# A two-block transformer kernel on one core: another order of work around the joined pair, and the joining copies on VectorE

## The chip, the cores and the metric

One Trainium2 chip, one of its cores. The metric is the device time of one execution in microseconds (us), the median of several runs. The engines are TensorE (PE, with its weight loads as PEld), VectorE (DVE), ScalarE (ACT), GpSimd (POOL) and SyncE (SP), which here issues nearly all the DMAs.

## The reference

256 tokens of width 1024 in float32 run through two layers of a first block (feed-forward, mixer, feed-forward) and two layers of a second one (mixer, cross attention, feed-forward). The change touches only the feed-forwards, of which there are six:

```
def swiglu_ffn(h, w_gate, w_up, w_down):
    return (jax.nn.silu(h @ w_gate) * (h @ w_up)) @ w_down
```

`h` is 256 x 1024, the hidden width is 2816, and every result is normalised and added to `x`.

## The kernel before

Every float32 product is made of three products of rounded parts: an operand is a high part (`w_hi`, `hT_hi`: rounded by a copy on ScalarE) and a low part (`w_lo`, `hT_lo`: operand minus high part, by a subtraction on VectorE), and TensorE multiplies high by high, high by low and low by high into the same PSUM bank. So each weight tile of 128 x 2048 passes through four hands: SyncE loads it into one of five `raw` buffers (`unit`, line 531), ScalarE makes its high part (`high`, line 1420, four buffers), VectorE its low part (`weight_low`, line 2112), and TensorE multiplies both in 24 matmuls of 512 columns (lines 738 and 875) and so frees them. Such a tile with its matmuls is a unit.

A feed-forward runs over 11 chunks of 256 hidden columns. A plain chunk has two units of gate and up weights, and one for the down projection, which TensorE multiplies one chunk later. Between them the hidden values are made: `silu` on ScalarE, `hidden` (the product with the up half) on VectorE, then the turning of the hidden tile by DMA transposes of 16-bit values. For it VectorE splits the float32 values into their upper and lower 16 bits (`part`, line 2208), SyncE issues two transposes (`turn_halves`, lines 571 and 567), and two copies of 128 x 512 uint16 put the halves together again in the buffer `joined` (`join_here` on ScalarE, line 1527, or `join` on VectorE, by the switch `JOIN_ON_ACT`). ScalarE rounds `joined` to the high part (`hidden_high`, line 1532), VectorE makes the low part (`hidden_low`, line 2203), and the down unit can be multiplied. `hidden` on ScalarE stands for `join_here` and `hidden_high` together.

Chunks 5 and 6 form a joined pair (`PAIRS = (5,)`): their gate and up products are made by seven smaller block products in place of eight, with sums of operands. VectorE makes the sums of rows (`rows_whole`, `row_sums`, `row_sums_low`, lines 2245 and 2247) during chunks 2 to 4, and the sums of weight blocks `t1` (line 2259), `t2` (2264), `t4` (2271) and `t3` (2275). TensorE multiplies the blocks in the order 1, 5, 2, 6, then the down unit of chunk 4, then 3, 7, 4. The text calls their units p1, p5, p2 and so on. `t1` needs p1 and p7 loaded, `t4` needs p2. `hold` (line 1585) copies the finished blocks 1 and 5 out of PSUM. Chunk 7 stands behind the pair (`chunk_behind`): TensorE multiplies its two units, then the down unit of chunk 5 (down 5) and that of chunk 6 (down 6). The hidden values of chunk 6 have buffers of their own: the halves in line 567, and `second_hi`, `second_lo`, which a profile shows as `form_lo`.

Each engine runs its instructions in the order in which they are written; nothing is scheduled at run time. So an engine that waits for one thing holds up all that is written behind it. The orders are in `chunk`, `chunk_behind` and `pair`, once for each engine. `low(n)` and `high(n)` below are the low and the high part of unit n of a feed-forward (11, 12: chunk 4; 13: down 3; 14: p1; 15: p5; 16: p2; 17: p6; 18: down 4; 24: down 5; 25: down 6; 26, 27: chunk 8; 28: down 7).

Of the kernel before, what the change touches and what calls it, by code (L numbers as in the profile page):

```python
# [45 lines left out]
AHEAD = HIGH_RING - 1  # L46
# [12 lines left out]


PAIRS = (5,)
JOIN_ON_ACT = True
HOOK = 7


# [140 lines left out]
def _program(ctx, nc, d, out, counted):  # L206
# [309 lines left out]
    def _(sp):  # L516
# [30 lines left out]
        def gate_up(L, k, kh, wg, wu, c):  # L547

            dst = raw[:, SLOT[L.unit(k)], :].rearrange("p (k g n) -> p k g n", k=4, g=2)
            halves = []  # L550
            for g, w in enumerate((wg, wu)):
                src = w[bass.ds(L.l, 1), 512 * kh:512 * kh + 512, bass.ds(c * FC, FC)]
                halves.append((dst[:, :, g, :], src.rearrange("o (k p) n -> p (o k) n", p=P)))
            unit(L, k, halves)
# [7 lines left out]
        def turn_halves(L, n, c):  # L562

            sp.wait_ge(halves_ready, L.turns(n, c))
            if c in SECOND:
                for t in range(TT):
                    sp.dma_start_transpose(second_halves_T[:, t, :, :],  # L567
                                           second_halves[:, t, :, :].rearrange("p b n -> p (b n)")).then_inc(second_turned, 16)
                return
            for t in range(TT):  # L570
                sp.dma_start_transpose(halves_T[:, t, :, :], halves[:, t, :, :].rearrange("p b n -> p (b n)")).then_inc(
                    halves_turned, 16)

        def ffn(L, n, k0, wg, wu, wd, ffn_ahead=None):
            for kh in range(2):
                gate_up(L, k0 + kh, kh, wg, wu, 0)
            if ffn_ahead:
                turn_halves(*ffn_ahead, NCHUNK - 1)

            def chunk(c):  # L580
                if c - 3 in PAIRS:
                    turn_halves(L, n, c - 3)
                    turn_halves(L, n, c - 2)
                gate_up(L, k0 + AT["gu", c, 0], 0, wg, wu, c)
                if c > 2 and c - 2 not in PAIRS and c - 3 not in PAIRS:
                    turn_halves(L, n, c - 2)
                gate_up(L, k0 + AT["gu", c, 1], 1, wg, wu, c)
                if c == 2:
                    turn_halves(L, n, 0)
                if c - 2 in PAIRS:  # L590
                    down(L, k0 + AT["down", c - 2], wd, c - 2)
                if c < NCHUNK - 2:
                    down(L, k0 + AT["down", c - 1], wd, c - 1)

            def pair(c):
                if c - 3 in PAIRS:
                    turn_halves(L, n, c - 3)
                    turn_halves(L, n, c - 2)
                square(L, k0 + AT["p", c, 1], wg, 0, c * FC)
                if c - 3 not in PAIRS:  # L600
                    turn_halves(L, n, c - 2)
                square(L, k0 + AT["p", c, 7], wu, 0, c * FC)
                square(L, k0 + AT["p", c, 3], wu, 512, c * FC)
                square(L, k0 + AT["p", c, 2], wg, 512, c * FC)
                turn_halves(L, n, c - 1)
                down(L, k0 + AT["down", c - 1], wd, c - 1)

            for c in range(1, NCHUNK - 1):
                if c in PAIRS:
                    pair(c)  # L610
                elif c not in SECOND:
                    chunk(c)
            end, c = k0 + U_FFN - 1, NCHUNK - 1
            for kh in range(2):
                gate_up(L, end - 4 + kh, kh, wg, wu, c)
            turn_halves(L, n, c - 2)
            for i in range(3):
                down(L, end - 2 + i, wd, c - 2 + i)
            turn_halves(L, n, c - 1)
# [789 lines left out]
    def _(act):  # L1409
        def high(L, k):  # L1410

            u = L.unit(k)
            if u >= UNITS:
                return
            if u not in FORMS:
                act.wait_ge(raw_landed[SLOT[u]], LANDED[u])
            if u >= HIGH_RING:
                act.wait_ge(unit_done, u - HIGH_RING + 1)
            src, dst = narrow_parts(u)[:2] if u in NARROW else (weight_of(u), w_hi[:, u % HIGH_RING, :])
            nc.scalar.activation(dst, src, ACT.Copy).then_inc(high_ready, 1)  # L1420
# [7 lines left out]
        def multiplied(L, k):  # L1428
            act.wait_ge(unit_done, L.unit(k) + 1)
# [80 lines left out]
        def ffn(L, n, j, k0):  # L1510
# [23 lines left out]
            def hidden(c, dst=bT_hi[:, KD:KD + 2, :]):  # L1534
                join_here(c)
                hidden_high(c, dst)
# [27 lines left out]
            def chunk_behind(k, c):  # L1564
                ahead = c + 1 in PAIRS
                high(L, k + 3)
                hidden(c - 2)
                if ahead:
                    form_high(c + 1, 1)
                else:  # L1570
                    high(L, k + 4)
                hidden(c - 1, second_hi)
                act.wait_ge(halves_ready, L.turns(n, c - 1))
                silu(L, k + 1, c, 4)
                if ahead:
                    form_high(c + 1, 5)
                    form_high(c + 1, 2)
                else:
                    high(L, k + 5)
                    high(L, k + 6)  # L1580

            def pair(k, c):
                def hold(dst, bank, number):
                    multiplied(L, k0 + AT["p", c, number])
                    nc.scalar.activation(dst, ps[:, bank, :], ACT.Copy).then_inc(*done("held", f"p{number}_{c}", f))

                form_high(c, 6)
                act.wait_ge(low_ready, pair_unit(L, k0, c, 5) + 1)
                act.wait_ge(*after("forms", f"t2_{c}", f))
                hold(held_1, 4, 1)  # L1590
                hold(held_5, 5, 5)
                multiplied(L, k0 + AT["down", c - 2])
                hidden(c - 1)
                high(L, k0 + AT["down", c - 1])
                form_high(c, 3)
                form_high(c, 7)
                multiplied(L, k0 + AT["p", c, 2])
                nc.scalar.activation(pair_hid[:, 0, :], ps[:, 4, :], ACT.Silu, scale=rstd_in[:, 0:1]).then_inc(silu_ready, 1)
                form_high(c, 4)
                for i in (8, 9, 10):  # L1600
                    high(L, k + i)
                act.wait_ge(*after("forms", f"c21_{c}", f))
                nc.scalar.activation(pair_hid[:, 1, :], sum_3, ACT.Silu, scale=rstd_in[:, 1:2]).then_inc(silu_ready, 1)
# [489 lines left out]
    def _(dve):  # L2093
# [97 lines left out]
        def ffn(L, n, j, k0):  # L2191
# [51 lines left out]
            def row_sums_low():  # L2243
                dve.wait_ge(*after("held", "rows_high", f))
                V.tensor_tensor(sum_lo_0, sums[:, 0:4, :], flat(sum_hi[:, 0:4, :]), ALU.subtract).then_inc(
                    *done("forms", "rows_low0", f))
                V.tensor_tensor(sum_lo_4[:, :, :], sums[:, 4:8, :], flat(sum_hi[:, 4:8, :]), ALU.subtract).then_inc(
                    *done("forms", "rows_low", f))
# [74 lines left out]

            def chunk(k, c):
                ahead = c + 1 in PAIRS
                join(c - 1)
                if not ahead:
                    weight_low(L, k + AHEAD)
                hidden_low(c - 1)
                if c + 3 == PAIRS[0]:  # L2330
                    rows_whole()
                if c + 2 == PAIRS[0]:
                    row_sums()
                if c + 1 == PAIRS[0]:
                    row_sums_low()
                if ahead:
                    t1(c + 1)
                    weight_low(L, k + AHEAD)
                else:
                    weight_low(L, k + 1 + AHEAD)  # L2340
                hidden(c)
                part(c)
                weight_low(L, k + (1 if ahead else 2) + AHEAD)

            def chunk_behind(k, c):
                ahead = c + 1 in PAIRS
                join(c - 2)
                weight_low(L, k + 3)
                hidden_low(c - 2)
                join(c - 1)  # L2350
                hidden_low(c - 1, second_hi, second_lo)
                if ahead:
                    t1(c + 1)
                weight_low(L, k + 4)
                hidden(c, 4)
                part(c)
                weight_low(L, k + 5)
                if not ahead:
                    weight_low(L, k + 6)
# [815 lines left out]
```

## Time and profile before

| | |
|---|---|
| time, median of 3 runs | 2059.15 us (2056.28 to 2060.22) |
| time of the profiled execution | 2059.28 us |
| span, first to last instruction | 2057.5 us |
| mean granted TensorE clock | 0.995 |
| PE busy | 2011.0 us (98%) |
| DVE busy | 1542.2 us (75%) |
| ACT busy | 1257.8 us (61%) |
| DMA | mean 192 GB/s |

Times in the trace count from the first instruction. A matmul's row lasts longer than the step to the next one, because they overlap. The six feed-forwards (FFN 1 to FFN 6) have their pair at about 83, 508, 695, 1121, 1527 and 1934 us.

### The profile page before, as it was taken

How to read it: one execution, taken by the hardware profiler on the slowest of the kernel's cores; microseconds unless marked ns; L12 is line 12 of the kernel's file. 1: busy time of each engine (PE TensorE's matmuls, PEld its weight loads, DVE VectorE, ACT ScalarE, POOL GpSimd, SP SyncE). 2: the span in 40 equal slices, each digit the busy share in tenths (PEclk: the TensorE clock that was granted, in tenths of full speed). 3: DMA queues.
4: the chain of work that ended last, by engine and by line, in shares of the span. 5: the costliest groups of instructions: out<-in, count | busy, mean ns of one | idle time of the engine just before them, and what ended most of it. 6: DMA issues, size and time to landing. Idle time of an engine off the chain costs nothing.

```text
span 2057.5 us, 24287 instructions
## 1 busy us (share of the span) xinstructions
PE 2011.0 (98%) x9442; PEld 1644.1 (80%) x9442; DVE 1542.2 (75%) x1892; ACT 1257.8 (61%) x1570; POOL 0.2 (0%) x4
## 2 busy tenths in 40 slices
PE   8999999999999999999999999999999999999998
PEld 6778887888787778887888788888887887888877
DVE  6776899777857776899767857876677578666774
ACT  6555657665657556667565656756656557566554
POOL 0000000000000000000000000000000000000000
PEclk9999999999999999999999999999999999999999
DMA  7756774567667755764567666554675674636654
GB/s 259 228 184 195 215 200 148 169 195 209 210 192 231 218 186 174 235 192 145 176 198 205 199 193 206 196 155 150 194 221 182 188 229 162 177 135 196 209 192 125
DMA packets 339123, 394.55 MB, mean 192 GB/s; under 512 B 123824, under 2 KB 235072, under 8 KB 339008
## 3 DMA queue, kind: packets, MB, share of 16 engines
q1 hardware_dynamic: 334912, 381.94, 60.4%
q10 hardware_dynamic: 4096, 11.05, 1.5%
q8 instruction: 75, 1.23, 0.2%
q14 instruction: 40, 0.33, 0.1%
HBM read 365.66 MB, written 1.05 MB: 178 GB/s over the span
## 4 chain that ended last, share of the span: by engine, by line
PE 79%; DVE 8%; DMA 4%; ACT 4%; issue 3%; SPq 2%; ACTq 0%; DVEq 0%
PE ps L738 68%; PE ps L875 4%; DMA raw<-in_ffn_w_up 2%; DVE w_lo L2112 2%; ACT w_hi L1420 1%; PE ps L809 1%; DVE scratch L2529 1%; ACT scratch L1527 1%; PE ps L1360 1%; SPq L567 1%; PE ps L1341 1%; DMA raw<-in_w_up 0%; DVE x L2162 0%; SPq L531 0%; DVE scratch L2284 0%
## 5 line engine op out<-in xcount | busy, mean ns | idle before, releaser
L2112 DVE TENSOR_TENSOR w_lo<-raw,w_hi 128x2048 fp32r<-128x2048 f32 x336 | 766.0, 2288 | 196.1 <-ACT w_hi L1420 194.0
L1420 ACT ACTIVATE w_hi<-raw 128x2048 fp32r<-128x2048 f32 (+2 forms) x340 | 642.9, 1897 | 392.8 <-PE ps L738 172.9
L738 PE MATMUL ps<-w_hi,hT_hi 128*128 128x512 f32 x1856 | 731.4, 394 | 0.0
L738 PE MATMUL ps<-w_lo,hT_hi 128*128 128x512 f32 x1856 | 723.5, 390 | 0.0
L738 PE MATMUL ps<-w_hi,hT_lo 128*128 128x512 f32 x1856 | 699.4, 389 | 0.0
L738 PEld LDWEIGHTS ps<-w_hi,hT_hi 128*128 128x128 f32 x1856 | 349.0, 188 | 76.0 <-issue 5.7
L738 PEld LDWEIGHTS ps<-w_hi,hT_lo 128*128 128x128 f32 x1856 | 348.4, 188 | 73.4
L738 PEld LDWEIGHTS ps<-w_lo,hT_hi 128*128 128x128 f32 x1856 | 349.1, 188 | 69.3
L738 PE MATMUL ps<-w_hi,bT_hi 128*128 128x512 f32 x608 | 240.1, 395 | 7.0 <-DVE bT_lo L2203 7.0
L738 PE MATMUL ps<-w_hi,bT_lo 128*128 128x512 f32 x608 | 237.0, 390 | 0.0
L738 PE MATMUL ps<-w_lo,bT_hi 128*128 128x512 f32 x608 | 236.8, 390 | 0.0
L738 PEld LDWEIGHTS ps<-w_hi,bT_hi 128*128 128x128 f32 x608 | 114.1, 188 | 37.3 <-DVE w_lo L2112 9.6
L738 PEld LDWEIGHTS ps<-w_hi,bT_lo 128*128 128x128 f32 x608 | 114.1, 188 | 24.3
L738 PEld LDWEIGHTS ps<-w_lo,bT_hi 128*128 128x128 f32 x608 | 114.2, 188 | 22.7
L1527 ACT ACTIVATE scratch<-scratch 128x512 uint16<-128x512 uint16 x132 | 92.3, 766 | 36.0 <-DMA scratch<-scratch 36.0
L2529 DVE SCALAR_TENSOR_TENSOR scratch<-scratch,pack 128x256 f32<-128x256 f32 x240 | 98.3, 478 | 0.1
L1659 ACT ACTIVATE scratch<-ps,stat 128x512 f32<-128x512 f32 (+1 forms) x84 | 51.3, 662 | 73.7 <-PE ps L738 73.5
L1516 ACT ACTIVATE scratch<-ps,stat 128x256 f32<-128x256 f32 x108 | 45.0, 468 | 81.3 <-PE ps L738 80.2
L2197 DVE SCALAR_TENSOR_TENSOR scratch<-ps,stat,scratch 128x256 f32<-128x256 f32 x108 | 47.2, 479 | 58.4 <-ACT scratch L1516 58.4
L1466 ACT ACTIVATE hT_hi<-ps,gains_T 128x128 fp32r<-128x128 f32 x192 | 53.5, 379 | 37.6 <-PE ps L809 36.5
L2203 DVE TENSOR_TENSOR bT_lo<-scratch,bT_hi 128x512 fp32r<-128x512 f32 x48 | 33.0, 687 | 42.8 <-ACT bT_hi L1532 42.6
L2135 DVE SCALAR_TENSOR_TENSOR hT_lo<-ps,gains_T,hT_hi 128x128 fp32r<-128x128 f32 x192 | 52.8, 343 | 11.3 <-ACT hT_hi L1466 11.3
(340 smaller groups left out, 1755.7 us busy)
## 6 DMA issues: line engine op xcount, KB each, us to landing
raw<-in_w_in SPq DMA_DIRECT2D x160, 512.0 KB, 4.7
raw<-in_ffn_w_down SPq DMA_DIRECT2D x88, 512.0 KB, 4.4
raw<-in_ffn_w_gate SPq DMA_DIRECT2D x86, 512.0 KB, 4.1
raw<-in_ffn_w_up SPq DMA_DIRECT2D x86, 512.0 KB, 5.0
raw<-in_w_gate SPq DMA_DIRECT2D x44, 512.0 KB, 4.0
raw<-in_w_up SPq DMA_DIRECT2D x44, 512.0 KB, 5.0
raw<-in_w_down SPq DMA_DIRECT2D x44, 512.0 KB, 4.4
raw<-in_w_out SPq DMA_DIRECT2D x32, 512.0 KB, 4.2
```

Source lines behind the costliest of these rows:

```text
L738: mm = nc.tensor.matmul(bank(t, half), act[:, tiles[i], t * P:(t + 1) * P], w, start=start and (i, n) == steps[0], stop=stop and (i, n) == ...
L875: mm = nc.tensor.matmul(ps[:, bank, :], act, w[:, i, :], start=start and (i, m) == (0, 0), stop=(i, m) == (3, 2), skip_group_check=True)
L1420: nc.scalar.activation(dst, src, ACT.Copy).then_inc(high_ready, 1)
L1466: nc.scalar.activation(hT_hi[:, 4 * kh + c, t * P:(t + 1) * P], ps[:, 6 - 2 * t + kh, c * P:(c + 1) * P], ACT.Copy, scale=pre_gain(L, j, 4 ...
L1516: silu_t = nc.scalar.activation(sil[:, t, :], ps[:, bank + t, 0:FC], ACT.Silu, scale=rstd_in[:, t:t + 1])
L1527: both = nc.scalar.activation(dst[:, t, :, :, :], src[:, t, :, :, :], ACT.Copy)
L1659: last = nc.scalar.activation(dst[:, t, :], src[:, t, :], func, scale=scale[:, t:t + 1])
L2112: V.tensor_tensor(lo, src, flat(hi), ALU.subtract).then_inc(low_ready, 1)
L2135: turned_low = V.scalar_tensor_tensor(hT_lo[:, c, t * P:(t + 1) * P], ps[:, 6 - 2 * t + kh, (c % 4) * P:(c % 4 + 1) * P], pre_gain(L, j, c ...
L2197: up = V.scalar_tensor_tensor(hid[:, t, :], ps[:, bank + t, FC:2 * FC], rstd_in[:, t:t + 1], sil[:, t, :], ALU.mult, ALU.mult)
L2203: V.tensor_tensor(lo, joined, flat(hi), ALU.subtract).then_inc(gT_ready, 1)
L2529: V.scalar_tensor_tensor(conv_y[:, c, :], src, w[:, c, i:i + 1], conv_y[:, c, :], ALU.mult, ALU.add).then_inc(*done("conv_taps", f"tap{i}_ ...
```

## The change

Six edits. The switch sends the joining copies to VectorE. On VectorE in the chunk ahead of the pair (chunk 4), `row_sums_low` moves from behind `hidden_low(3)` to the head, and the low part of p5 moves ahead of `hidden(4)`. In `chunk_behind`, VectorE takes `hidden_low(5)` ahead of the low part of unit 25, and ScalarE rounds chunk 6's hidden values before it rounds unit 26. In the pair ScalarE rounds the down unit of chunk 4 before the hidden values of that chunk. On SyncE the first load of chunk 8 moves between the transposes of chunk 5 and of chunk 6.

```diff
-JOIN_ON_ACT = True
+JOIN_ON_ACT = False
@@ sync, ffn: chunk(c)
                 if c - 3 in PAIRS:
                     turn_halves(L, n, c - 3)
+                gate_up(L, k0 + AT["gu", c, 0], 0, wg, wu, c)
+                if c - 3 in PAIRS:
                     turn_halves(L, n, c - 2)
-                gate_up(L, k0 + AT["gu", c, 0], 0, wg, wu, c)
                 if c > 2 and c - 2 not in PAIRS and c - 3 not in PAIRS:
                     turn_halves(L, n, c - 2)
@@ scalar, ffn: chunk_behind(k, c)
                 high(L, k + 3)
                 hidden(c - 2)
+                hidden(c - 1, second_hi)
                 if ahead:
                     form_high(c + 1, 1)
                 else:
                     high(L, k + 4)
-                hidden(c - 1, second_hi)
@@ scalar, ffn: pair(k, c)
                 hold(held_5, 5, 5)
+                high(L, k0 + AT["down", c - 1])
                 multiplied(L, k0 + AT["down", c - 2])
                 hidden(c - 1)
-                high(L, k0 + AT["down", c - 1])
@@ vector, ffn: chunk(k, c)
                 ahead = c + 1 in PAIRS
+                if c + 1 == PAIRS[0]:
+                    row_sums_low()
                 join(c - 1)
                 if not ahead:
                     weight_low(L, k + AHEAD)
...
-                if c + 1 == PAIRS[0]:
-                    row_sums_low()
                 if ahead:
                     t1(c + 1)
                     weight_low(L, k + AHEAD)
-                else:
-                    weight_low(L, k + 1 + AHEAD)
+                weight_low(L, k + 1 + AHEAD)
                 hidden(c)
                 part(c)
-                weight_low(L, k + (1 if ahead else 2) + AHEAD)
+                if not ahead:
+                    weight_low(L, k + 2 + AHEAD)
@@ vector, ffn: chunk_behind(k, c)
                 join(c - 2)
+                hidden_low(c - 2)
                 weight_low(L, k + 3)
-                hidden_low(c - 2)
```

VectorE in FFN 1 before the change, from the low part of chunk 3's hidden values (`bT_lo`) to the low parts of p2 and p6 (the last two rows):

```order
L2203 TENSOR_TENSOR bT_lo<-scratch,bT_hi 128x512
L2245 TENSOR_TENSOR sp<-scratch,sum_hi 128x1024
L2247 TENSOR_TENSOR sum_lo<-scratch,sum_hi 128x1024
L2259 TENSOR_TENSOR scratch<-raw 128x2048
L2112 TENSOR_TENSOR w_lo<-raw,w_hi 128x2048
L2197 SCALAR_TENSOR_TENSOR scratch<-ps,stat,scratch 128x256 x2
L2208 COPY scratch<-scratch 128x1024
L2112 TENSOR_TENSOR form_lo<-scratch,w_hi 128x2048
L2264 TENSOR_TENSOR scratch<-raw,scratch 128x2048
L2271 TENSOR_TENSOR scratch<-raw,scratch 128x2048
L2112 TENSOR_TENSOR w_lo<-raw,w_hi 128x2048
L2112 TENSOR_TENSOR form_lo<-scratch,w_hi 128x2048
```

The same stretch of the changed kernel, whose line numbers are one higher:

```order
L2246 TENSOR_TENSOR sp<-scratch,sum_hi 128x1024
L2248 TENSOR_TENSOR sum_lo<-scratch,sum_hi 128x1024
L2223 COPY scratch<-scratch 128x2x2x128 x2
L2204 TENSOR_TENSOR bT_lo<-scratch,bT_hi 128x512
L2260 TENSOR_TENSOR scratch<-raw 128x2048
L2113 TENSOR_TENSOR w_lo<-raw,w_hi 128x2048
L2113 TENSOR_TENSOR form_lo<-scratch,w_hi 128x2048
L2198 SCALAR_TENSOR_TENSOR scratch<-ps,stat,scratch 128x256 x2
L2209 COPY scratch<-scratch 128x1024
L2265 TENSOR_TENSOR scratch<-raw,scratch 128x2048
L2272 TENSOR_TENSOR scratch<-raw,scratch 128x2048
L2113 TENSOR_TENSOR w_lo<-raw,w_hi 128x2048
```

The row sums now lead, two joining copies stand behind them, and the low part of p5 (`form_lo<-scratch,w_hi`) stands ahead of the hidden values.

ScalarE in FFN 1 behind the pair before the change, where `form_lo` is the high part of chunk 6's hidden values and the first `w_hi` row is the high part of unit 26:

```order
L1527 ACTIVATE scratch<-scratch 128x2x2x128 x2
L1532 ACTIVATE bT_hi<-scratch 128x512
L1420 ACTIVATE w_hi<-raw 128x2048
L1527 ACTIVATE scratch<-scratch 128x2x2x128 x2
L1532 ACTIVATE form_lo<-scratch 128x512
L1516 ACTIVATE scratch<-ps,stat 128x256 x2
```

The same stretch of the changed kernel:

```order
L1533 ACTIVATE bT_hi<-scratch 128x512
L1533 ACTIVATE form_lo<-scratch 128x512
L1421 ACTIVATE w_hi<-raw 128x2048
L1517 ACTIVATE scratch<-ps,stat 128x256 x2
L1421 ACTIVATE w_hi<-raw 128x2048 x3
```

The four copies have left ScalarE, and the high part of unit 26 comes after both hidden tiles.

## Rows read from the trace of the kernel before

**Rows 1.** What TensorE waited for, by line and releaser: total us, times, longest

```profile
PE ps L738 <- DVE form_lo L2203: 12.8, 6, 2.3
PE ps L875 <- DVE w_lo L2112: 8.3, 6, 3.1
PE ps L738 <- DVE bT_lo L2203: 7.0, 14, 0.8
```

**Rows 2.** Timeline of TensorE, FFN 2, around the start of block 2

```profile
521.89 0.40 PE L875 MATMUL ps<-w_hi,sum_lo 128*128 128x512 f32 x1
523.32 0.47 PE L875 MATMUL ps<-w_hi,hT_hi 128*128 128x512 f32 x1 [1.03 <-DVE w_lo L2112]
523.63 0.40 PE L875 MATMUL ps<-w_lo,hT_hi 128*128 128x512 f32 x1
523.86 0.40 PE L875 MATMUL ps<-w_hi,hT_lo 128*128 128x512 f32 x1
```

**Rows 3.** Timeline of TensorE, FFN 2, starts of down 4, 5, 6

```profile
529.76 0.47 PE L738 MATMUL ps<-w_hi,bT_hi 128*128 128x512 f32 x1 [0.65 <-DVE bT_lo L2203]
...
555.03 0.47 PE L738 MATMUL ps<-w_hi,bT_hi 128*128 128x512 f32 x1 [0.33 <-DVE bT_lo L2203]
...
562.92 0.47 PE L738 MATMUL ps<-w_hi,form_lo 128*128 128x512 f32 x1 [2.17 <-DVE form_lo L2203]
```

**Rows 4.** Windows behind waits: length, busy us, then granted clock, DMA share, GB/s

```profile
99.40:102.70 3.30, 3.30 (x10) 2.53 (x9) 3.30 (x2) 3.03 (x2) 0.00 (x0) 0.50 0.05 15
...
1176.60:1180.00 3.40, 3.40 (x16) 2.78 (x15) 3.37 (x5) 3.10 (x2) 0.00 (x0) 1.00 0.80 264
...
1990.50:1993.60 3.10, 3.10 (x9) 2.43 (x8) 3.06 (x5) 2.56 (x2) 0.00 (x0) 0.50 0.73 229
```

**Rows 5.** Groups by line: joining copies on ACT, and the like on DVE

```profile
L1527 ACT ACTIVATE scratch<-scratch 128x512 uint16<-128x512 uint16 x132 | 92.3, 766 | 36.0 <-DMA scratch<-scratch 36.0
L2441 DVE COPY scratch<-scratch 128x512 uint16<-128x512 uint16 x12 | 4.6, 461 | 4.7 <-DMA scratch<-scratch 4.7
```

**Rows 6.** Timeline of VectorE, FFN 2: bT_lo, t1, low(16), low(18); low(24) with low(25)

```profile
504.46 0.69 DVE L2203 TENSOR_TENSOR bT_lo<-scratch,bT_hi 128x512 fp32r<-128x512 f32 x1 [4.43 <-ACT bT_hi L1532]
...
507.56 2.29 DVE L2259 TENSOR_TENSOR scratch<-raw 128x2048 f32<-128x2048 f32 x1
...
520.89 2.28 DVE L2112 TENSOR_TENSOR w_lo<-raw,w_hi 128x2048 fp32r<-128x2048 f32 x1
...
526.73 2.29 DVE L2112 TENSOR_TENSOR w_lo<-raw,w_hi 128x2048 fp32r<-128x2048 f32 x1 [1.35 <-ACT w_hi L1420]
...
549.80 4.49 DVE L2112 TENSOR_TENSOR w_lo<-raw,w_hi 128x2048 fp32r<-128x2048 f32 x2
```

**Rows 7.** Timeline of ScalarE: FFN 2, and one row of FFN 4

```profile
516.68 1.92 ACT L1420 ACTIVATE w_hi<-raw 128x2048 fp32r<-128x2048 f32 x1 [4.15 <-DMA raw<-in_ffn_w_gate]
...
522.32 0.60 ACT L1585 ACTIVATE scratch<-ps 128x512 f32<-128x512 f32 x1 [1.31 <-PE ps L875]
...
558.19 1.92 ACT L1420 ACTIVATE w_hi<-raw 128x2048 fp32r<-128x2048 f32 x1 [5.88 <-DMA raw<-in_ffn_w_up]
...
1131.14 1.92 ACT L1420 ACTIVATE w_hi<-raw 128x2048 fp32r<-128x2048 f32 x1 [5.27 <-DMA raw<-in_ffn_w_gate]
```

**Rows 8.** SyncE in FFN 2: p7 and p3, then chunk 6's transposes

```profile
500.49 6.32 SPq L531 DMA_DIRECT2D raw<-in_ffn_w_up  x4
...
549.91 2.50 SPq L567 DMA_TRANSPOSE scratch<-scratch  x2
```

**Rows 9.** DMA issues by target: count, KB each, median us from issue to landing

```profile
raw<-in_ffn_w_up SPq DMA_DIRECT2D x86, 512.0 KB, 5.0
...
scratch<-scratch SPq DMA_TRANSPOSE x168, 2.8
```

**Rows 10.** FFN 4, its start: VectorE's memory work, ScalarE's joining copies

```profile
1069.62 2.48 DVE L2708 TENSOR_TENSOR bT_lo<-ps,bT_hi 128x512 fp32r<-128x512 f32 x4 [0.20 <-ACT bT_hi L1847]
...
1072.21 1.41 ACT L1527 ACTIVATE scratch<-scratch 128x512 uint16<-128x512 uint16 x2 [1.15 <-DMA scratch<-scratch]
```

## The prediction

> **What bounds the kernel now.** The list of waits comes first, because TensorE is 98% busy: what it waited for is nearly all that can be won. Three rows make up nearly all of its waiting: the low part of chunk 6's hidden values (`form_lo`), 12.8 us in 6 waits; the low part of p2 (`w_lo` at line 875), 8.3 us in 6, of them 3.1 in one FFN; and the low part of other hidden values (`bT_lo`), 7.0 us in 14 [rows 1]. Next, the timeline of TensorE around one wait, for what a wait costs beside its idle time. Matmuls step by 0.23 us; block 2 began at 523.32, and the way from the matmul before it to the one behind it took 1.74 us instead of 0.46, so 1.28 us were lost for an idle time of 1.03 [rows 2]. I add 0.25 to each wait. FFN 2 shows the other three places: 0.65 at down 4, 0.33 at down 5, 2.17 at down 6 [rows 3]. Last, the windows behind the waits: in some the granted clock is 0.50, 1.2 GHz instead of 2.4, and in others, as in FFN 4, it stays at 1.00 [rows 4]. At 0.50 only 10 and 9 matmuls touch 3.3 and 3.1 us, where 16 touch 3.4 us at 1.00 [rows 4]. From the same timeline I count some 8 slow matmuls behind each of five waits: p2 in FFN 1, down 6 in FFN 1, 2, 3 and 6. Each such fall costs 8 x 0.2 = 1.6 us.
>
> So the pair now costs, over six FFNs:
> - p2: 8.3 + 6 x 0.25 + one fall of 1.6 = 11.4
> - down 4 (five FFNs): 5 x (0.65 + 0.25) = 4.5
> - down 5: 6 x (0.33 + 0.25) = 3.5
> - down 6: 12.8 + 6 x 0.25 + four falls = 20.7
>
> Together 40.1 us. The rest of the `bT_lo` row, 7.0 - 5 x 0.65 - 6 x 0.33 = 1.8, lies in three waits for the first down unit of FFN 1, 3 and 6: 2.5 us with the additions.
>
> **The switch.** 132 copies leave ScalarE at 0.77 us each, 101 us in all. VectorE's nearest copy, of the same elements and type for another pair of transposed halves, takes 0.46 [rows 5]: 61 us come to VectorE, which is 75% busy. The two copies of one chunk cost 0.92 instead of 1.41. Bounds: 0.46 and ScalarE's 0.77, so 0.92 to 1.54 a chunk; I take the first, from the same engine. What is queued behind `join` on VectorE is a low part that TensorE needs about one chunk later. In plain chunks VectorE waits for ScalarE anyway, so I cost the copies there at nothing; without that cover each chunk would lose up to 0.9.
>
> **VectorE ahead of the pair** (times of FFN 2). Until `bT_lo` at 504.46 VectorE stood idle for 4.43 us [rows 6]. Now the row sums (two of 1.2 us) fill this: from 500.0 to 502.4. Then join to 503.3, ScalarE's 0.63, `bT_lo` to 504.7. `t1` was at 507.56 [rows 6]; it needs p7, issued first of the four half loads from 500.49, its second half some 0.4 later; with 5.0 us to land that is 505.9 [rows 8, 9]. So `t1` runs from 505.9 to 508.1, 1.7 us earlier. low(14) and low(15) follow to 512.5 (2.2 us each, as in the pair of low parts that takes 4.49 [rows 6]), then hidden(4), its split (1.5 us together) and `t2` to 516.2. `t4` needs p2, which landed at 516.68 [rows 7], and ends at 518.9; low(16) ends at 521.1 instead of 523.1. TensorE could have started at 523.32 - 1.03 = 522.29 [rows 2]. The wait at p2 goes.
>
> **The pair.** low(17) to 523.3, join to 524.2. The high part of down 4 now stands ahead of the hidden values: it follows `hold`, which ended at 522.9 before and ends the same now, since it waits for TensorE's block 5 [rows 7], and runs to 524.8. low(18) was at 526.73, after 1.35 us of waiting for ScalarE [rows 6]; it is now at 524.8 to 527.0, then `bT_lo` to 527.7. TensorE, 1.28 earlier from p2 on, wants down 4 at 529.76 - 0.65 - 1.28 = 527.8 [rows 3]. This wait goes too, with nothing to spare.
>
> **Behind the pair** (in times of before; what follows TensorE moves with it). low(24) from 549.80 to 552.0, then join(5) to 552.9, ScalarE to 553.6, `bT_lo` to 554.3; it no longer stands behind low(25). TensorE wants it at 555.03 - 0.33 = 554.7 [rows 3, 6]: the wait goes. low(25) to 556.5. The wait at down 6 came from ScalarE: it stood at high(26) until a load landed at 558.19 and only then joined chunk 6 [rows 7]. In the new order chunk 6's halves need only their transposes. Those were issued at 549.91 and take 2.50 to issue [rows 8]; with one load of two halves (1.1 us of issue) before them they end at about 553.0 and land, 2.8 after issue [rows 9], at 554.6. join(6) at 556.5 to 557.4, ScalarE to 558.1, low part to 558.8. TensorE wants it at 562.92 - 2.17 - 0.58 = 560.2 [rows 3]: 1.4 us to spare. The wait goes, and the fall of the clock with it. Next in line is unit 26, wanted another 5.4 us later: its high part follows at 558.1 and its low part ends at 562.3, covered.
>
> **What stays.** In FFN 4, p2 landed at 1131.14 [rows 7], 1.2 us after TensorE had begun the pair (FFN 2: at once), so `t4` comes no earlier than 1131.2: I leave 0.2 of waiting at p2 and 0.15 at down 4, with the additions 0.9. FFN 1 has the wait of 3.1 [rows 1]; the advance is at most that of FFN 2, 2.0, and I take 1.8: 1.3 stay at p2 and 0.15 at down 4, with the additions 2.0, and no fall of the clock (behind 1.03 there was none, behind 2.17 there was).
>
> **What it costs.** FFN 4 has at its start VectorE's four low parts of the memory, 1069.62 to 1072.10, while the transposed halves land at 1072.21 [rows 10]. In the code `join(0)` now stands ahead of these four, so they begin at 1073.1 and `bT_lo` ends at 1076.3. TensorE began down 0 at 1075.56 without waiting: a new wait of 0.7 + 0.25. At the other starts the chain is 0.5 shorter, for three waits 1.5.
>
> **Sum.** -40.1 + 0.9 + 2.0 + 0.9 - 1.5 = -37.8. The profiled execution took 2059.3 us, the median of the runs 2059.15. That gives 2021.5 us.
>
> **A rule on the order of transfers.** The rows show that transposes land 2.8 us after issue in the median [rows 9], whatever runs beside them. The Trainium skill, DMA: Bandwidth & Descriptors, section Queues, rings and completion order, says that each DMA engine consumes the descriptors of one issuing engine's queue in the order of its ring; so the transposes of chunk 6 would begin only behind the load that is now ahead of them. That speaks against the edit on SyncE. By the row the edit costs nothing, by the rule up to the 7.5 us of rival 1 below, whose times are worked out there from rows.
>
> **Rivals.**
> 1. The transposes of chunk 6 land late. Their load is issued until 550.2 and lands at about 554.7 (5.0 after issue), in bad cases 1.5 later (p2 in FFN 4). If the transposes only start then, they land 2.8 later, 557.5 to 559.0; the low part comes at 559.8 to 561.3, so TensorE waits nothing to 1.1 us. Six waits of 1.0 with the addition: +7.5, 2029. For it: the load does go ahead. Against it: in the trace the transposes of chunk 4 follow p2's load in the same way.
> 2. VectorE has no room in the pair. down 4 has nothing to spare. Were the copies 0.77 each, or `t1` no earlier, p2 and down 4 would keep most of their waits: +8 to +11, about 2031.
> 3. Slower than before. VectorE waits inside `join(6)`, and low(26), hidden(7) and low(27) stand behind it. This eats the whole gain of 6.3 us per FFN only if the transposes land past 556.5 + 1.4 + 6.1 = 564, 14 us after their issue, five times the median. About 2062.
> 4. No change. The waits at down 6 go but come back elsewhere, because the stream of weights sets the pace. Against it: ScalarE and VectorE idle for us at a time behind TensorE.
>
> **Chances and range.** Forecast 0.72, rival 1 0.10, rival 2 0.11, rival 3 0.04, rival 4 0.03. A change below 0.2%, 4 us, can't be told from none here. Faster 0.93, same 0.03, slower 0.04. Below, the sum can't pass 2059.3 - 40.1 - 2.5 = 2016.7; above, rivals 1 and 2 end at about 2031, with some 3 us for both in part: 2016 to 2034. The forecast's own range is 2017 to 2027.
>
> **What would show it.** Right: no `form_lo` row among TensorE's waits; the `w_lo` row at line 875 near 1.5 us, in FFN 1 and 4 alone; the clock at 0.50 only at the very start; copies of 0.46 us on VectorE; low(16) 2 us earlier against block 1. Wrong: a `form_lo` row with VectorE's join released by a DMA (rival 1), `w_lo` or `bT_lo` waits in all six FFNs (rival 2). The wait of 0.7 us at FFN 4's down 0 should be new.

## The result, and the profile after

The changed kernel takes 2022.91 us in the median of four runs (2022.12 to 2023.40), the kernel before 2057.72 us (2054.05 to 2060.22) beside it. The ratio is 0.9832, with a 95% interval of 0.9815 to 0.9849. The forecast was 2021.5: 1.4 us off as a time, 3.0 off as a gain (37.8 forecast, 34.8 measured), because the kernel before came out 1.4 us below the 2059.15 that the forecast starts from. That the time is so near is in part luck.

The head of the page of the changed kernel: span, then busy time, share and instructions of each engine.

```profile
span 2021.6 us, 24239 instructions
PE 2000.0 (99%) x9442; PEld 1639.1 (81%) x9442; DVE 1589.3 (79%) x2024; ACT 1169.2 (58%) x1438; POOL 0.2 (0%) x4
```

What TensorE waited for in the changed kernel; it answers to [rows 1]:

```profile
PE ps L876 <- DVE w_lo L2113: 2.1, 2, 1.8
...
PE ps L739 <- DVE bT_lo L2204: 0.5, 1, 0.5
```

The `form_lo` row is gone. Of the 12.8 + 8.3 + 7.0 us of before, 2.6 are left in this list: p2 in FFN 1 (1.82) and FFN 4 (0.28), and one new wait at the start of FFN 4 (0.46). The first matmul behind each of the three, from the timeline of TensorE:

```profile
97.54 0.47 PE L876 MATMUL ps<-w_hi,hT_hi 128*128 128x512 f32 x1 [1.82 <-DVE w_lo L2113]
...
1055.50 0.47 PE L739 MATMUL ps<-w_hi,bT_hi 128*128 128x512 f32 x1 [0.46 <-DVE bT_lo L2204]
...
1115.96 0.47 PE L876 MATMUL ps<-w_hi,hT_hi 128*128 128x512 f32 x1 [0.28 <-DVE w_lo L2113]
```

The window behind the longest of them answers to the first of [rows 4]: 15 matmuls in 3.4 us at a clock of 1.00 (the number behind POOL's `0.00 (x0)`), where 10 matmuls touched 3.3 us at 0.50.

```profile
97.50:100.90 3.40, 3.36 (x15) 2.79 (x16) 3.40 (x4) 2.41 (x2) 0.00 (x0) 1.00 0.90 311
```

The joining copies, now on VectorE, answer to [rows 5]; they take 0.45 us each, and 63.8 us of the idle time ahead of them is waiting for the transposes:

```profile
L2223 DVE COPY scratch<-scratch 128x512 uint16<-128x512 uint16 x132 | 52.7, 454 | 63.8 <-DMA scratch<-scratch 63.8
```

The rows of VectorE in FFN 2 answer to [rows 6]. They are `t1`, the low part of p5, `t4`, the low part of p2, the join, the low part of down 4 and `bT_lo`; then, behind the pair, the join and the low part of chunk 6:

```profile
498.74 2.29 DVE L2260 TENSOR_TENSOR scratch<-raw 128x2048 f32<-128x2048 f32 x1 [1.16 <-DMA raw<-in_ffn_w_up]
...
503.15 2.29 DVE L2113 TENSOR_TENSOR form_lo<-scratch,w_hi 128x2048 fp32r<-128x2048 f32 x1
...
509.78 2.29 DVE L2272 TENSOR_TENSOR scratch<-raw,scratch 128x2048 f32<-128x2048 f32 x1 [0.55 <-DMA raw<-in_ffn_w_gate]
511.99 2.29 DVE L2113 TENSOR_TENSOR w_lo<-raw,w_hi 128x2048 fp32r<-128x2048 f32 x1
...
516.39 0.80 DVE L2223 COPY scratch<-scratch 128x512 uint16<-128x512 uint16 x2
517.93 2.29 DVE L2113 TENSOR_TENSOR w_lo<-raw,w_hi 128x2048 fp32r<-128x2048 f32 x1 [0.74 <-ACT w_hi L1421]
520.14 0.69 DVE L2204 TENSOR_TENSOR bT_lo<-scratch,bT_hi 128x512 fp32r<-128x512 f32 x1
...
548.22 0.80 DVE L2223 COPY scratch<-scratch 128x512 uint16<-128x512 uint16 x2 [0.22 <-DMA scratch<-scratch]
549.71 0.69 DVE L2204 TENSOR_TENSOR form_lo<-scratch,form_lo 128x512 fp32r<-128x512 f32 x1 [0.70 <-ACT form_lo L1533]
```

The low part of chunk 6's hidden values ends at 550.40, and TensorE takes it at 551.49, in step. `bT_lo` ends at 520.83, and TensorE takes it at 520.97, not quite in step: down 4 begins 0.37 us behind the matmul before it, where 0.23 is the step. The list of waits does not show this.

```profile
520.60 0.39 PE L876 MATMUL ps<-w_hi,sp 128*128 128x512 f32 x1
520.97 0.47 PE L739 MATMUL ps<-w_hi,bT_hi 128*128 128x512 f32 x1
...
551.49 0.40 PE L739 MATMUL ps<-w_hi,form_lo 128*128 128x512 f32 x1
```

**Where the time went.** Both traces have 9442 matmuls in the same order, so one can be laid on the other matmul by matmul: each place where the distance between the two starts changes is a place where time was won or lost. The last matmul comes 35.9 us earlier, which is the whole difference of the spans (2057.5 and 2021.6). The places, each from two matmuls before its first one to 22 behind it, in us (rounded), beside what the terms of the prediction's sum come to:

```
place                              measured   predicted
p2, six FFNs                         -8.8       -9.4
down 4                               -3.3       -3.7
down 5                               -3.3       -3.5
down 6                              -20.4      -20.7
first down unit of FFN 1, 3, 6       -1.9       -1.5
first down unit of FFN 4             +0.7       +0.95
all else                             +1.1        0
sum                                 -35.9      -37.8
```

### The profile page after: what moved, and what is told of

Its sections match the earlier page's. It is cut to its first block, busy times and chain, and to the rows that moved or that the text cites. A ratio compares the mean times of both kernels' runs of the same rounds, so it can differ in the third digit from the quotient of the medians.

```text
span 2021.6 us, 24239 instructions
## 1 busy us (share of the span) xinstructions
PE 2000.0 (99%) x9442; PEld 1639.1 (81%) x9442; DVE 1589.3 (79%) x2024; ACT 1169.2 (58%) x1438; POOL 0.2 (0%) x4
## 4 chain that ended last, share of the span: by engine, by line
PE 88%; DVE 6%; DMA 2%; ACT 2%; issue 1%; SPq 1%; ACTq 0%; DVEq 0%
PE ps L739 75%; PE ps L876 5%; DVE w_lo L2113 2%; PE ps L810 1%; DVE scratch L2530 1%; DMA raw<-in_ffn_w_up 1%; PE ps L1361 1%; PE ps L1342 1%; DVE x L2163 0%; ACT w_hi L1421 0%; DMA raw<-in_w_co 0%; DVE scratch L2567 0%; PE ps L925 0%; PE ps L833 0%; DMA x<-in_x 0%
## 5 line engine op out<-in xcount | busy, mean ns | idle before, releaser
L2223 DVE COPY scratch<-scratch 128x512 uint16<-128x512 uint16 x132 | 52.7, 454 | 63.8 <-DMA scratch<-scratch 63.8
L1533 ACT ACTIVATE bT_hi<-scratch 128x512 fp32r<-128x512 f32 x48 | 30.2, 629 | 72.3 <-DVE scratch L2223 72.2
```

Of the source, the lines that this page charges most:

```text
L1533: nc.scalar.activation(dst, joined, ACT.Copy).then_inc(gT_hi_ready, 1)
L2223: both = V.tensor_copy(dst[:, t, :, :, :], src[:, t, :, :, :])
```

## The experiments

All but the first are the changed kernel with something altered. Each was timed beside the kernel before, whose median was 2057.7 to 2062.3 us in the five sets; its time is set against the changed kernel's 2022.9, so a difference of a us or two says nothing by itself. What a place costs comes from the matmuls laid over those of the changed kernel.

**The switch by itself.** The kernel before with `JOIN_ON_ACT = False` and nothing else.

```diff
-JOIN_ON_ACT = True
+JOIN_ON_ACT = False
```

> The kernel before with the joining copies on VectorE and nothing else. My theory: the order of work brings the gain, and the switch alone loses. In the pair join(4) ends at about 525.6 in FFN 2's times, ScalarE rounds the hidden values to 526.3 and only then down 4, to 528.2, so VectorE's low parts end at about 531: a wait of some 3 us at down 4 in each FFN, instead of 0.65, some with a fall of the clock; at p2 about 0.3 instead of 1.0, at down 5 about 1.1 instead of 0.3, at down 6 about 1.7 instead of 2.1. Time 2060 to 2072 us, slower than before or the same. Rival (the copies on VectorE bring the gain, since they relieve ScalarE): 2035 us or less, and the wait at down 6 below 0.5.

Measured: 2059.95 us (2056.97 to 2062.59, 11 runs), ratio 1.0003 [0.9994, 1.0011]: no difference. Two shifts cancel. At down 6 the wait of [rows 3] shrinks from 2.17 to 0.13 us, where some 1.7 were expected. ScalarE still stands at the late load, but the halves are joined by then, so from the load to the low part it takes 3.2 us in place of 4.6; and TensorE arrives later, because it has lost time at down 4 and down 5. Against the kernel before this place gives -18.5 us over six FFNs, the slow matmuls behind the waits included.

```profile
558.45 1.92 ACT L1420 ACTIVATE w_hi<-raw 128x2048 fp32r<-128x2048 f32 x1 [4.79 <-DMA raw<-in_ffn_w_up]
560.27 0.61 ACT L1532 ACTIVATE form_lo<-scratch 128x512 fp32r<-128x512 f32 x1
```

At down 4, where the kernel before lost 0.9 in five of the FFNs, there is now this (TensorE, and VectorE with what is ahead of it):

```profile
528.38 0.72 PE L738 MATMUL ps<-w_hi,bT_hi 128*128 128x512 f32 x1 [2.61 <-DVE bT_lo L2203]
```

```profile
521.99 0.79 DVE L2222 COPY scratch<-scratch 128x512 uint16<-128x512 uint16 x2
525.34 2.29 DVE L2112 TENSOR_TENSOR w_lo<-raw,w_hi 128x2048 fp32r<-128x2048 f32 x1 [2.56 <-ACT w_hi L1420]
527.55 0.69 DVE L2203 TENSOR_TENSOR bT_lo<-scratch,bT_hi 128x512 fp32r<-128x512 f32 x1
```

ScalarE did the hidden values first, and these now wait for VectorE's join, so down 4's high part ends 2.56 us too late for VectorE. This place costs 18.6 us more than before, down 5 4.0 more, and p2 and the starts give some 3.5 back. The time came out just below the 2060 to 2072 expected.

**The order by itself.** The changed kernel with the copies on ScalarE again (`JOIN_ON_ACT = True`).

> The changed kernel with the copies back on ScalarE. My theory: no wait comes back in the pair or behind it (down 4 ready at the same time, down 5 and down 6 ready earlier than in the changed kernel), the first down unit waits some 0.5 us longer in three FFNs and 0.5 us less in FFN 4. Time 2021 to 2026 us, within 0.2% of the changed kernel. Rival (the switch brings part of the gain): over 2030 us, with waits for bT_lo or form_lo in all six FFNs.

Measured: 2023.17 us (2020.59 to 2023.79, 5 runs), ratio 0.9826 [0.9813, 0.9839]; its last matmul comes 0.05 us earlier than the changed kernel's. The order brings all of the gain, and the switch nothing that the times can show, with the new order either. The places show a little: with the copies on ScalarE the first down units wait 1.27, 0.68 and 0.28 us in FFN 1, 3 and 6, and FFN 4's new wait is gone, 1.7 us in all for the switch, which other places of this one trace take back. ScalarE's 92.4 us of copies and VectorE's 52.7 both lie beside waiting.

**ScalarE's edit in the pair undone.**

```diff
-                high(L, k0 + AT["down", c - 1])
                 multiplied(L, k0 + AT["down", c - 2])
                 hidden(c - 1)
+                high(L, k0 + AT["down", c - 1])
```

> The changed kernel with one edit undone: ScalarE rounds chunk 4's hidden values before down 4 again. My theory: since join(4) now stands on VectorE behind the low part of p6, ScalarE can round down 4 only from 524.9 on, and TensorE waits about 2 us at down 4 in each FFN, in some with a fall of the clock of 1.6 us. Time 2034 to 2046 us. Rival (the high part of down 4 is hidden): 2023 us.

Measured: 2040.82 us (2039.54 to 2041.24, 4 runs), ratio 0.9914 [0.9900, 0.9927]: 17.9 us more than the changed kernel, all of it at down 4 (4.1, 2.1, 1.8, 4.3, 2.3 and 3.4 in FFN 1 to 6). The windows behind the waits of FFN 4 and FFN 5, with the granted clock behind POOL's `0.00 (x0)`:

```profile
1132.40:1135.80 3.40, 3.37 (x9) 2.70 (x10) 3.40 (x2) 1.28 (x1) 0.00 (x0) 0.60 0.00 0
...
1537.20:1540.60 3.40, 3.39 (x15) 2.85 (x16) 3.40 (x2) 1.30 (x1) 0.00 (x0) 1.00 0.00 0
```

The waits are 2.59 and 2.25 us, and only the first is followed by a stretch at 1.2 GHz. With the copies on VectorE this edit is the dearest to leave out, although the kernel before lost only 4.5 us here: it pays for what the switch would break. What it is worth with the copies on ScalarE, no run here shows.

**Both edits on chunk 6's way undone**, ScalarE's in `chunk_behind` and SyncE's.

```diff
-                hidden(c - 1, second_hi)
...
                     high(L, k + 4)
+                hidden(c - 1, second_hi)
@@ sync
                     turn_halves(L, n, c - 3)
-                gate_up(L, k0 + AT["gu", c, 0], 0, wg, wu, c)
-                if c - 3 in PAIRS:
                     turn_halves(L, n, c - 2)
+                gate_up(L, k0 + AT["gu", c, 0], 0, wg, wu, c)
```

> The changed kernel with the two edits behind the pair undone: high(26) before chunk 6's hidden values on ScalarE, both transposes before the load of unit 26 on SyncE. My theory: the wait at down 6 is for this load through ScalarE. It comes back as 1.2 to 1.7 us in each FFN (the copies are shorter than on ScalarE), mostly without a fall of the clock. Time 2030 to 2038 us. Rival (the wait at down 6 was cured by moving the copies): 2023 us.

Measured: 2032.32 us (2030.46 to 2032.54, 4 runs), ratio 0.9871 [0.9858, 0.9885]: 9.8 us at down 6, 1.5 to 1.8 in each FFN. The chain of [rows 7] is back: ScalarE stands 4.82 us for the load and rounds chunk 6 behind it, and TensorE waits. It is half of the 20.4 us that this place gave: the waits are 1.25 to 1.58 us where they were 2.03 to 2.25, and none is followed by a stretch at 1.2 GHz, where four were.

```profile
550.21 1.92 ACT L1420 ACTIVATE w_hi<-raw 128x2048 fp32r<-128x2048 f32 x1 [4.82 <-DMA raw<-in_ffn_w_up]
552.03 0.61 ACT L1532 ACTIVATE form_lo<-scratch 128x512 fp32r<-128x512 f32 x1
...
553.51 0.47 PE L738 MATMUL ps<-w_hi,form_lo 128*128 128x512 f32 x1 [1.44 <-DVE form_lo L2203]
```

**Each of the two undone alone**, first ScalarE's, then SyncE's.

> The changed kernel with only ScalarE's edit behind the pair undone (high(26) before chunk 6's hidden values; the load of unit 26 stays ahead of the transposes). My theory: the load lands about 2.3 us earlier than in the kernel before, ScalarE is through with high(26) at about the time at which VectorE has joined chunk 6, and the low part comes some 1 us before TensorE wants it: no wait at down 6, 2022 to 2025 us. Rival (ScalarE's order is what counts): a form_lo wait of 1 us or more in each FFN, 2030 us or more.

Measured for ScalarE's alone: 2022.53 us (2021.29 to 2023.16, 4 runs), ratio 0.9811 [0.9795, 0.9828].

> The changed kernel with only SyncE's edit undone (both transposes before the load of unit 26). My theory: ScalarE no longer needs the load before chunk 6's hidden values, so nothing waits: 2022 to 2025 us. With this and the run that undoes ScalarE's edit alone both at no cost, either edit would be enough, and only both undone bring the wait back. Rival (the earlier load is needed): waits at unit 26 or down 6, over 2027 us.

Measured for SyncE's alone: 2023.17 us (2022.37 to 2024.01, 4 runs), ratio 0.9815 [0.9800, 0.9830]. Neither costs anything: either edit does the whole work. With the old order on ScalarE, the load is issued ahead of the transposes and lands 0.2 us behind the start of down 5 in FFN 2, where with both edits undone it lands 3.7 behind it, so that the rounding of unit 26 ends before join(6) does:

```profile
545.22 1.92 ACT L1421 ACTIVATE w_hi<-raw 128x2048 fp32r<-128x2048 f32 x1 [1.31 <-DMA raw<-in_ffn_w_up]
547.59 0.63 ACT L1533 ACTIVATE form_lo<-scratch 128x512 fp32r<-128x512 f32 x1 [0.44 <-DVE scratch L2223]
```

**VectorE's edit behind the pair undone**: the low part of unit 25 ahead of chunk 5's hidden values.

```diff
-                hidden_low(c - 2)
                 weight_low(L, k + 3)
+                hidden_low(c - 2)
```

> The changed kernel with VectorE's edit behind the pair undone: the low part of unit 25 again ahead of the low part of chunk 5's hidden values. In the changed kernel the join of chunk 5 ends at 544.4 us in FFN 2, the hidden values' low part runs from 545.10 to 545.8 and TensorE starts down 5 at 545.94 with 0.06 us of waiting. Behind the low part of unit 25 (544.3 to 546.6) the hidden values would come at 547.2: a wait of 1.3 us for bT_lo, no fall of the clock, 1.3 to 1.5 us in each of six FFNs, 7.5 to 9 us: about 2031. Rival, as the prediction's sum had it (0.33 plus 0.25 for each FFN): 3.5 us, 2026.4. Down 6 should stay free of waiting in both.

Measured: 2030.49 us (2030.37 to 2031.27, 4 runs), ratio 0.9861 [0.9845, 0.9878]. The distance grows by 1.0 to 1.3 us at down 5 in each FFN, 7.4 in all; no other wait is new. The kernel before lost only 3.5 here, since ScalarE joined the halves beside VectorE's low parts. With the two copies (0.79 us) between VectorE's low parts the wait grows, as it did with the switch alone (1.01 us idle at this place). So the edit is worth more in the new kernel than the wait of before that it took away.

**p5's low part back behind `hidden(4)`** on VectorE.

```diff
-                weight_low(L, k + 1 + AHEAD)
+                else:
+                    weight_low(L, k + 1 + AHEAD)
                 hidden(c)
                 part(c)
-                if not ahead:
-                    weight_low(L, k + 2 + AHEAD)
+                weight_low(L, k + (1 if ahead else 2) + AHEAD)
```

> The changed kernel with p5's low part back behind hidden(4) on VectorE. My theory: low(15), t2, t4 and low(16) come about 1.3 us later, the wait at p2 is about 0.3 us in each FFN and down 4 waits about 0.2: with the additions some 1 us per FFN, 2027 to 2031 us. Rival (VectorE has room there): 2023 us.

Measured: 2028.50 us (2028.48 to 2028.90, 4 runs), ratio 0.9841 [0.9827, 0.9856], a time in the range expected, with longer waits at p2 than the 0.3 us expected and none at down 4. p2 has its wait in all six FFNs (2.21 in FFN 1, then 1.07, and 0.71 to 0.72), and this place costs 6.6 us. In four of them the list of waits names ScalarE's `hold`, which ends at the same time as p2's low part; in the changed kernel TensorE starts p2 while the same `hold` still runs, so it is the low part that counts. Behind the first of them the clock falls (0.69 in the mean of the window), where it does not behind the 1.82 of the changed kernel:

```profile
97.90:101.30 3.40, 3.40 (x11) 2.70 (x12) 3.40 (x4) 0.99 (x3) 0.00 (x0) 0.69 0.39 138
```

**The row sums back behind `hidden_low(3)`.**

```diff
-                if c + 1 == PAIRS[0]:
-                    row_sums_low()
                 join(c - 1)
...
+                if c + 1 == PAIRS[0]:
+                    row_sums_low()
                 if ahead:
```

> The changed kernel with row_sums_low back behind hidden_low(3). My theory: with the copies on VectorE bT_lo is ready at about 503.8 in FFN 2's times, the row sums then end at about 506.1, and t1, which needs p7 at 505.7, starts at most 0.5 us later: 2022 to 2026 us. Rival (this edit brings the 2 us at p2): w_lo waits of 1 us in all FFNs, 2029 us or more.

Measured: 2022.58 us (2021.97 to 2023.23, 4 runs), ratio 0.9812 [0.9797, 0.9827]. This edit is worth nothing beside the switch. With the join no longer behind the sums, `bT_lo` is ready 0.7 us earlier than in the changed kernel. In FFN 2 the sums behind it end 0.4 us after the load of p7 is there, and `t1` begins straight behind them, 0.6 us later against block 1 than in the changed kernel. p2's low part had more room than that. `t1` of FFN 2 in this run:

```profile
498.77 2.29 DVE L2260 TENSOR_TENSOR scratch<-raw 128x2048 f32<-128x2048 f32 x1
```

With the copies on ScalarE the edit may well count: in the order by itself `bT_lo` comes 1.4 us later against block 1 than here, and the sums behind it would push `t1` back to where it was before. That is an estimate from these two traces; no run here shows it.

**Every joining copy made twice** in four of the six FFNs (1, 2, 5, 6): once more into a part of the scratch that nothing reads, so nothing of what is computed changes.

```diff
...
+                again = scratch[:, SCRATCH - 512:SCRATCH].bitcast(U16).rearrange("p (i t n b) -> p t b i n", i=2, t=TT, b=2)
+                for to in (again, dst) if L.b or L.l < DEPTH - 1 else (dst,):
...
```

> The changed kernel with each joining copy made a second time into an unused buffer, in FFN 1, 2, 5 and 6 (88 copies more, 0.40 to 0.46 us each, 0.9 us a chunk). My theory: hidden in plain chunks; at down 4 and at down 5 of these four FFNs there is nothing to spare, so about 0.4 and 0.9 us of waiting appear there, and nothing in FFN 3 and 4: 2027 to 2031 us. Rival (VectorE's time is on the path throughout): 88 x 0.42 = 37 us more, 2060 us. Rival (the pair has room): 2023 us.

Measured: 2031.06 us (2030.13 to 2032.03, 4 runs), ratio 0.9862 [0.9849, 0.9876]: 88 copies more, and the last matmul 7.4 us later, at the upper end of what was expected. So a copy of 0.45 us costs nothing at its first making, but the cover is thin: each one added costs 0.08 us in the mean, at down 4, down 5 and the first down units (0.2 to 0.8 each), and once, behind the pair of FFN 1, 1.4.

**Both loads of chunk 8 ahead of chunk 6's transposes** on SyncE.

```diff
                 gate_up(L, k0 + AT["gu", c, 0], 0, wg, wu, c)
-                if c - 3 in PAIRS:
-                    turn_halves(L, n, c - 2)
...
                 gate_up(L, k0 + AT["gu", c, 1], 1, wg, wu, c)
+                if c - 3 in PAIRS:
+                    turn_halves(L, n, c - 2)
```

> The changed kernel with both loads of chunk 8 ahead of chunk 6's transposes. By the rule of ring order the transposes land behind both: some 3 us later than in the changed kernel, of which 1.4 us are spare, so a form_lo wait of 1 to 2 us in each FFN, in some with a fall of the clock: 2031 to 2045 us. If transposes pass the loads they land 2.8 us after issue (1.1 us later than now): no wait, 2023 us.

Measured: 2031.72 us (2029.20 to 2035.06, 4 runs), ratio 0.9866 [0.9852, 0.9880]. The `form_lo` wait is back in all six FFNs (6.5 us; 7.8 by the distance at down 6, and 1.2 more once, behind the pair of FFN 1), and now VectorE's join is released by the transfer, 2.60 us late:

```profile
552.57 0.80 DVE L2223 COPY scratch<-scratch 128x512 uint16<-128x512 uint16 x2 [2.60 <-DMA scratch<-scratch]
```

How long chunk 6's transposes take from issue to landing, the shortest, the median and the longest of twelve: in the kernel before, with no load ahead of them, in the changed kernel, with one (of two halves), and in this kernel, with two:

```profile
DMA to landing us min/median/max: 2.3/2.3/2.4
```

```profile
DMA to landing us min/median/max: 4.1/4.7/5.2
```

```profile
DMA to landing us min/median/max: 5.1/6.2/7.2
```

In FFN 2 of the changed kernel the load ahead of them landed at 547.11 and they at 547.67 and 548.19; with two loads ahead, the last landed at 551.51 and they at 552.03 and 552.54. Of the 168 transposes of each kernel none landed before a load that was issued ahead of it on SyncE, and none less than 0.2 us behind. The Trainium skill, DMA: Bandwidth & Descriptors, section Queues, rings and completion order, says that a DMA engine takes one issuer's descriptors in ring order; the landings agree.

**The memory first.** In FFN 4 `join(0)` goes behind the memory's four low parts, the new wait's cause.

```diff
-                join(0)
                 if n:
                     memory_low(L.l)
+                join(0)
```

> The changed kernel with join(0) of FFN 4 behind the four low parts of the memory on VectorE. My theory: TensorE's wait at FFN 4's down 0 (0.5 us with 0.2 more) goes, nothing else moves: 0.7 us less in the span, which the times can't tell from the changed kernel. Rival: the wait stays, because the transposed halves land late.

Measured: 2021.26 us (2020.80 to 2022.54, 5 runs), ratio 0.9816 [0.9803, 0.9830]. The `bT_lo` row of 0.5 us is gone from TensorE's waits, and -0.74 us stand at this place; the rest of the difference of 1.65 is scattered over the whole trace and no larger than what separates two runs of one kernel. VectorE does the memory while it would wait for the transposes:

```profile
1047.74 2.48 DVE L2709 TENSOR_TENSOR bT_lo<-ps,bT_hi 128x512 fp32r<-128x512 f32 x4 [0.21 <-ACT bT_hi L1848]
1050.27 0.80 DVE L2223 COPY scratch<-scratch 128x512 uint16<-128x512 uint16 x2
```

## Why the prediction was right, step by step

- **The bound.** Right: TensorE's waits were what could be won. 0.25 us beside each idle time held (2.07 for 1.82 in FFN 1, 1.25 to 1.29 for 1.0 at down 5 with VectorE's edit undone). Of it 0.17 is how the idle time is counted, from the end of a row of 0.40 us, where the step is 0.23; the rest is that the next matmul comes 0.08 late.
- **The switch at nothing.** Right, shown by the order alone, and copies of 0.45 us against 0.46 taken. What the prediction did not say is that the switch without the new order moves the wait from down 6 to down 4 and ends at no change.
- **VectorE ahead of the pair.** Right in result, not in every cause. In FFN 2 low(16) began 4.3 us behind block 1 before and 2.2 behind it after, 2.1 earlier (2 forecast). The earlier `t1` alone does not do it: with p5's low part back behind the hidden values low(16) began 4.3 behind block 1 again, though `t1` was as early as in the changed kernel. The row sums, with which the step began, are worth nothing beside the switch.
- **p2, the term that was most off.** -8.8 in place of -9.4, nearly all of it in FFN 1, where the step "I take 1.8: 1.3 stay" was too kind: 1.82 stayed. There `t1` began at 82.39 in place of 82.97, only 0.6 us earlier, because it then waited for its load. VectorE works all but without a pause from it to the end of p2's low part at 97.4. Taking the hidden values later saved 0.6 more, and the wait shrank by 1.3. No fall of the clock, as forecast. FFN 2 gave 1.30 where 1.28 was in the sum.

```profile
82.97 2.29 DVE L2259 TENSOR_TENSOR scratch<-raw 128x2048 f32<-128x2048 f32 x1
```

```profile
82.39 2.29 DVE L2260 TENSOR_TENSOR scratch<-raw 128x2048 f32<-128x2048 f32 x1 [1.67 <-DMA raw<-in_ffn_w_up]
```

- **down 4 with nothing to spare.** Nearly right: `bT_lo` comes 0.14 us too late to be taken in step, which costs 0.23 in five FFNs and 0.15 in FFN 4. In FFN 1 it is a loss that the kernel before did not have (0.4 forecast there and in FFN 4, nothing in the other four). Hence -3.3 in place of -3.7. Rival 2 was close, as copies made twice show.
- **down 5.** -3.3 in place of -3.5: 0.6 each in five FFNs, and 0.3 in FFN 2, where TensorE still waits 0.06.
- **down 6.** Right in size (-20.4 against -20.7), and the wait did come from the load ahead of ScalarE's rounding. Two edits take it away and either is enough; the prediction credited ScalarE's alone and put SyncE's down as harmless at best.
- **Transposes in 2.8 us.** Wrong: behind one load they take 4.1 to 5.2 us. Rival 1 had the mechanism right but its price too high: in FFN 2 they landed 0.6 and 1.1 us behind the load, where it counted 2.8. The rule on the order of transfers held against the median of [rows 9], in which transposes with and without loads ahead are mixed. That it cost nothing is in part luck: VectorE is busy with unit 25 until 548.0 anyway, so the join starts 0.2 us late in FFN 2 and in time elsewhere. 1.1 us of slack are left in FFN 2 and 1.5 in the others, where 1.4 were forecast. Two loads ahead go past it.
- **What it costs.** The wait at FFN 4's start came, 0.46 us and 0.7 by the distance, forecast 0.7 and 0.95; the memory first takes it away.
- **The starts** gave 1.9 in place of 1.5.

The sum was 1.9 us too high. The terms account for some 0.9 of it, p2 in FFN 1 and down 4 the most; the other 1.1 lies at the very start and in places that the change does not touch, where two runs differ by as much, and stays unexplained.

## What to carry to other kernels

Undo the edits of a reordering one at a time in the new kernel: their worths (in the medians 17.9, 7.6, 5.6, and 9.4 for two that replace each other) add up to some 40 us for a gain of 35, since each holds a place that the others have made tight. Undo them in twos as well: two of the seven moves, the switch and the row sums, are worth nothing alone, and by the numbers above they may replace each other as the two behind the pair do. A median landing time over all transfers of a kind hides the queue: take the landing with the same things issued ahead of it. And where an engine stands for a transfer, put there the work that needs no transfer, as with the memory in FFN 4.

## What was unexpected of the hardware

The clock of TensorE after a wait of some 2 us is not settled by the wait's length. Over all kernels here, leaving out the first 10 us of each, the nine waits of 2.57 us and more were each followed by a stretch at 1.2 GHz. Of the nine from 2.0 to 2.3 us five were: in the kernel before, one of 2.157 at down 6 of FFN 1 was and one of 2.153 at the same place of FFN 4 was not. Of those below 1.9 us one of 1.80 was, and none of 1.83, 1.82, 1.77 and 1.75. A wait with such a stretch cost 1.7 to 1.9 us beside its idle time, one without 0.25 to 0.4. What else decides stayed open.
